# Mixture-of-experts blocks made of two half blocks of 32 slots, four weight slots in the ring, and a TensorE loop of one block

## The chip, the cores and the metric

The kernel runs on one core of a Trainium2 chip. The metric is the device time of one execution in microseconds (us), as the median of three runs. In the profile, PE is TensorE (PEld its weight loads, PEldq its sequencer's own instructions), DVE is VectorE, ACT ScalarE, POOL GpSimd and SP SyncE.

## The reference

A backbone of two layers works on 256 latent tokens and 256 context tokens of width 1024. Each layer has a token mixing part (windowed attention, a bidirectional state-space scan, a bidirectional gated recurrence and global attention, side by side) and a channel mixing part, which the change touches:

```python
scores = jax.nn.sigmoid((h @ router_w).astype(jnp.float32))
...
_, idx = lax.top_k(jnp.where(expert_mask, biased, -jnp.inf), TOP_K)
w = w / jnp.sum(w, axis=-1, keepdims=True) * ROUTED_SCALE
shared = (jax.nn.silu(h @ sh_gate) * (h @ sh_up)) @ sh_down
return routed_experts(h, idx, w, w_gate, w_up, w_down) + shared
```

Each token goes to 8 of 64 experts. An expert is `(silu(x @ w_gate) * (x @ w_up)) @ w_down` with a hidden width of 256, so it has 3 MB of f32 weights. The first layer routes 512 tokens, the second only the 256 latent ones, since only those are put out.

## The kernel before

After the routing, VectorE sorts the assignments of tokens to experts into blocks of 64 slots. A block holds tokens of one expert; an expert with 65 tokens takes two blocks, and what is left of its last block is empty. The table `TAB` holds the expert of every block, `PEND` the running sum of blocks by expert, and `NPR` the number of pairs of blocks. Each engine then runs a loop over pairs of blocks, whose two halves are written out (u = 0 and 1) so that each can use its own buffers: `OH`, `XGT`, `HIDT`, `YSB`, `XG`, and the banks 0/1 for up, 2/3 for down, 4/6 for turned tokens.

For block b the work runs as follows. VectorE builds a one-hot matrix of the block's slots (`one_hot`, L1631) from the table's expert. TensorE multiplies it with `KV` (`meta`, L1185), which gives token numbers and destinations. VectorE turns these into row numbers (`rows`, L1641). GpSimd gathers the token rows by an indirect DMA (L657), each token as two half rows, so that 64 slots fill 128 partitions. TensorE transposes them (`turn_tokens`, L1196), and ScalarE copies them to `XGT` (L885). TensorE multiplies them with the gate and the up weights (`up`, L1202: 8 chunks, the gate to partitions 0 to 63 and up to 64 to 127 of one bank, as two column groups of 64). ScalarE takes silu of the gate half (L891), VectorE multiplies (`product`, L1676), TensorE transposes the hidden rows (`turn_hidden`, L1225), ScalarE copies them (L902), TensorE multiplies with the down weights (`down`, L1217, two column groups of 64), ScalarE evicts (L907), and GpSimd scatters the rows to `yrows` (L676).

TensorE's order in the body is: `meta` of block b+3, up of b+1 with the hidden transpose of b inside it, the token transposes of b+2, down of b. Table loads (`expert_of`) and branches choose the ring slot of the expert, since addresses in the code are fixed: there is a copy of up and of down for each of the three slots (L1260 to L1278).

The weights arrive through a ring of three slots of 3 MB. Expert e lies in slot e % 3. SyncE loads gate, up and down of an expert (L521, L526) on one queue, in order of experts. In `reload` (L529) it waits until the last block of the expert in that slot is through up (`pe_gu`), issues the gate and up loads of the expert three further on, waits for its down (`pe_dn`), and issues the down load. One semaphore per slot counts the landings, and up waits for all three of them (`expert_landed`, L1213). All 64 experts are loaded, with tokens or not. The ring also serves the adaLN, projection and shared-expert weights before; expert 2's slot is the last to come free, after the shared expert's down.

Ahead of the loop VectorE counts blocks by expert in `NB` (L1608 to L1610), prepares blocks 0 to 2, and computes the tokens' expert weights `WK` and their diagonals `DG` (L1669, L1673) before the first `product`.

## Time and profile before

| | |
|---|---|
| median of 3 runs | 2148.57 us (2148.31 to 2156.99) |
| the profiled execution | 2138.5 us |
| its span | 2136.7 us |
| mean granted clock of TensorE in it | 0.948 of full speed |
| TensorE busy | 1835.1 us (86% of the span) |
| VectorE, ScalarE, GpSimd busy | 846.2, 542.0, 426.2 us |
| moved by DMA | 578.28 MB, mean 271 GB/s |

The busy times are of one profiled execution, so they are read against its span and not against the median. Busy shares are means over stages of different kinds; the two expert loops are stretches of their own in it. The idle time that a view gives ahead of a group of instructions is split by what ended it: a DMA, another engine's line, or "issue", when the engine waited for nothing that the profile shows.

### The profile page before, as it was taken

What the parts mean: (1) busy time and instruction counts of PE and PEld (TensorE: products, weight loads), DVE (VectorE), ACT (ScalarE), POOL (GpSimd) and SP (SyncE); (2) the same over time, 40 slices, a digit from 0 to 9 for tenths busy, and PEclk for the clock granted to TensorE, in tenths of its full rate; (3) what the DMA queues carried; (4) which work ended last, traced back from release to release, by engine and by line L of the source; (5) the groups of instructions that cost most, each with busy time, mean ns of one, the idle gap of its engine ahead of it and who ended that gap; (6) DMA issues with size and microseconds to landing.
All of it is one profiled execution on the core that took longest, in us unless ns stands there. A gap on an engine that the chain in (4) does not pass through costs nothing. (4 is left out here: it accounts for less than half of the span.)

```text
span 2136.7 us, 39465 instructions
## 1 busy us (share of the span) xinstructions
PE 1835.1 (86%) x11495; PEld 992.2 (46%) x11496; DVE 846.2 (40%) x2836; ACT 542.0 (25%) x1163; POOL 426.2 (20%) x417
## 2 busy tenths in 40 slices
PE   4999699879999999999997589879688887888885
PEld 3545454435445545445553355545444444444442
DVE  2245563363333333333334526543532323223334
ACT  2142352222222222222221214233222222222221
POOL 0001300012223223222321000130122222222220
PEclk8999899999999999999999889969799999999998
DMA  8315510449999789897985853631599999999994
GB/s 278 126 66 201 188 60 1 177 170 377 369 388 357 257 309 359 315 376 270 383 334 198 297 158 110 250 129 34 209 354 370 409 399 411 397 406 400 363 385 185
DMA packets 170400, 578.28 MB, mean 271 GB/s; under 512 B 29756, under 2 KB 34592, under 8 KB 153448
## 3 DMA queue, kind: packets, MB, share of 16 engines
q1 hardware_dynamic: 134592, 515.49, 62.7%
q0 software_dynamic: 29056, 60.07, 7.7%
q10 hardware_dynamic: 6696, 1.98, 0.4%
q8 instruction: 35, 0.57, 0.1%
q14 instruction: 21, 0.17, 0.0%
HBM read 565.73 MB, written 45.75 MB: 286 GB/s over the span
## 5 line engine op out<-in xcount | busy, mean ns | idle before, releaser
L1208 PE MATMUL bank<-arena 128*64 128x256 f32 x5120 | 643.0, 395 | 124.8 <-DMA arena<-in_exp_w_down 81.5
L1208 PEld LDWEIGHTS bank<-arena 128*64 128x64 f32 x5120 | 353.0, 140 | 293.1 <-DMA arena<-in_exp_w_down 86.8
L676 POOL DMA_INDIRECT yrows<-arena x158 | 160.3, 1014 | 832.8 <-ACT arena L907 814.7
L1221 PE MATMUL bank<-arena 128*64 128x512 f32 x1264 | 306.5, 606 | 0.7 <-issue 0.5
L657 POOL DMA_INDIRECT arena<-hrows,arena x164 | 185.9, 1133 | 144.3 <-DVE arena L1650 91.6
L1680 DVE TENSOR_TENSOR arena<-arena,bank 64x256 f32<-64x256 f32 x160 | 68.0, 425 | 353.9 <-ACT arena L891 353.8
L902 ACT ACTIVATE arena<-bank 128x128 f32<-128x128 f32 x158 | 44.2, 280 | 565.6 <-PE bank L1227 565.6
L907 ACT ACTIVATE arena<-bank 128x512 f32<-128x512 f32 x158 | 94.4, 597 | 210.1 <-PE bank L1221 210.1
L973 PE MATMUL bank<-arena 128*128 128x512 f32 (+3 forms) x384 | 133.9, 512 | 11.7 <-DVE arena L1337 11.7
L1645 DVE COPY arena<-bank 128x3 f32<-128x3 f32 x164 | 26.4, 161 | 288.9 <-PE bank L1192 288.3
L1199 PE MATMUL bank<-arena 128*128 128x128 f32 x648 | 121.9, 311 | 7.8 <-DMA arena<-hrows,arena 7.8
L1221 PEld LDWEIGHTS bank<-arena 128*64 128x64 f32 x1264 | 76.9, 136 | 110.7 <-issue 92.1
L1199 PEld LDWEIGHTS bank<-arena 128*128 128x128 f32 x648 | 90.9, 209 | 70.5 <-issue 61.2
L885 ACT ACTIVATE arena<-bank 128x512 f32<-128x512 f32 x162 | 96.8, 597 | 55.8 <-PE bank L1199 55.5
L973 PEld LDWEIGHTS bank<-arena 128*128 128x128 f32 x384 | 79.0, 217 | 64.8 <-issue 45.8
L1638 DVE TENSOR_TENSOR arena<-arena 128x512 bf16<-128x512 f32 (+1 forms) x166 | 97.9, 590 | 5.7
L976 PE MATMUL bank<-arena 128*128 128x512 f32 (+1 forms) x256 | 100.0, 552 | 0.0
L891 ACT ACTIVATE arena<-bank 64x256 f32<-64x256 f32 x160 | 60.2, 376 | 127.4 <-PE bank L1208 127.4
L1192 PEld LDWEIGHTS bank<-arena 128*128 128x128 bf16 x518 | 24.2, 97 | 133.3 <-issue 133.2
L1127 PE MATMUL bank<-arena 128*128 128x512 f32 x192 | 82.9, 593 | 1.0 <-DVE arena L1517 1.0
L1636 DVE TENSOR_SCALAR arena<-arena 128x4 f32 (+1 forms) x166 | 38.3, 231 | 108.1 <-issue 106.5
L1227 PEld LDWEIGHTS bank<-arena 64*128 64x128 f32 x316 | 48.9, 201 | 62.1 <-issue 62.1
(297 smaller groups left out, 1834.1 us busy)
## 6 DMA issues: line engine op xcount, KB each, us to landing
arena<-in_exp_w_gate SPq DMA_DIRECT2D x128, 1024.0 KB, 8.8
arena<-in_exp_w_up SPq DMA_DIRECT2D x128, 1024.0 KB, 11.1
arena<-in_exp_w_down SPq DMA_DIRECT2D x128, 1024.0 KB, 9.0
arena<-in_w_ada SPq DMA_DIRECT2D x10, 3072.0 KB, 13.7
arena<-yrows SPq DMA_DIRECT2D x24, 1024.0 KB, 16.3
arena<-in_w_ada SPq DMA_DIRECT2D x8, 2048.0 KB, 9.9
arena<-in_w_in SPq DMA_DIRECT2D x8, 2048.0 KB, 18.8
arena<-in_w_out SPq DMA_DIRECT2D x4, 2048.0 KB, 12.1
```

The lines of the kernel that those rows point to most:

```text
L657: pool.indirect_dma_start(out=XG[k], out_offset=None, in_=hrows, in_offset=bass.IndirectOffsetOnAxis(ap=GIX[k], axis=0), bounds_check=2 * ...
L676: pool.indirect_dma_start(out=yrows, out_offset=bass.IndirectOffsetOnAxis(ap=SIXS[u], axis=0), in_=YSB[u], in_offset=None, bounds_check=2 ...
L885: act.activation(XGT[b_par], bank[(4, 6)[b_par]][:, :].rearrange("p (c h s) -> p c h s", c=4, h=2), ACT.Copy).then_inc(a_xe, 1)
L907: act.activation(YSB[u], bank[2 + u][:, :], ACT.Copy).then_inc(a_y, 1)
L973: ins = pe.matmul(bank[o % 4][:, c0:width], HT[:, c, tile_of(j)], w[:, c, c0:], start=(c == 0), stop=(c == 7))
L976: ins = pe.matmul(bank[o % 4][:, c0:], w[:, c, tile_of(j)], HT[:, c, c0:], start=(c == 0), stop=(c == 7))
L1127: ins = pe.matmul(bank[2 * t + hf][:, :], MT[:, c, tile_of(t)], w[:, c, :], start=(c == 0), stop=(c == 7))
L1199: ins = pe.transpose(bank[(4, 6)[b_par]][:, c * P:(c + 1) * P], XG[b_par][:, c:512:4], IDENT)
L1208: ins = pe.matmul(bank[b_par][64 * gu:64 * gu + 64, 0:HID], XGT[b_par][:, c, hh, :], wv[:, gu, hh, c, :], start=(c8 == 0), stop=(c8 == 7))
L1221: ins = pe.matmul(bank[2 + b_par][64 * cg:64 * cg + 64, :], HIDT[b_par][:, c, :], wv[:, c, cg * 512:(cg + 1) * 512], start=(c == 0), stop= ...
L1638: dve.tensor_tensor(OH[par][:, T0:], IOTA.unsqueeze(1).broadcast_to([P, NTS, P]), RR[:, T0:].unsqueeze(2).broadcast_to([P, NTS, P]), ALU.i ...
L1680: dve.tensor_tensor(HIDB[64:128, :], HS[64:128, :], bank[par][64:128, 0:HID], ALU.mult).then_inc(v_hid, 1)
```

## The change

A block still has 64 slots, but it is now two units of 32 slots, each with an expert of its own. Tokens are rounded up to 32 per expert; an expert without tokens gets one unit. The number of blocks is half the number of units, rounded up to an even number. `TAB` holds the expert of each unit, and the new `TABK` the sum of the two experts of a block; since they are the same expert or neighbours, half the sum gives the first and the remainder the step to the second.

Up writes four column groups of 32 (gate and up of both units), down four as well (two halves of the output for both units), so each has twice the matmuls, of 32 stationary columns. `meta` writes two halves with a copied `KVP`, which `one_hot` fills on VectorE.

The ring has four slots, the fourth in the region of `H`, which is free once the rows have been stored. The down landings have a semaphore of their own (`sp_dn`), so up waits only for the gate and up parts. Experts 0, 1, 3, 2 are loaded ahead, 3 after the shared expert's up products and the store of the rows.

TensorE's loop holds one block for two. `OH`, `XGT`, `HIDT` and the banks 0, 2 and 4 are single now; up of b+1 waits for product(b) before it starts, and `turn_hidden` stands after 4 of the 8 chunks for 6. Each of up and down has eight copies: four slots, with or without a step.

```diff
-SLOTS = 64
+UNIT = 32
+SLOTS = 2 * UNIT
...
-        ring = [rRING + 6144 * k for k in range(3)]
+        ring = [rRING + 6144 * k for k in range(3)] + [rH]
...
                 def reload(i, u):
...
+                    units_up_to = sp.value_load(TABP[0:1, bass.ds(i * NSLOT + u, 1)], min_val=0, max_val=MAXU)
+                    used = sp.snap((units_up_to + 1) // 2)
+                    sp.wait_ge(sp_land[u], i * 32 + (base_land[u] + 32))
+                    sp.wait_ge(sp_dn[u], i * 16 + 16)
...
-                for e in range(3):
-                    sp.wait_ge(*done_of[P_OUT + e])
+                for e in (0, 1, 3, 2):
+                    if e < 3:
+                        sp.wait_ge(*done_of[P_OUT + e])
+                    else:
+                        sp.wait_ge(pe_sh, 4)
+                        sp.wait_ge(pool_hr, 16 * NTS)
                     load_up(e, e)
                     load_down(e, e)
...
                     for t in TS:
-                        ins = pe.matmul(bank[7][:, 0:3], OH[b_par][:, t, :], KV[:, t, bass.ds(e, 1), :].rearrange("p a c -> p (a c)"),
-                                        start=(t == T0), stop=(t == NT - 1))
+                        for un in range(2):
+                            ins = pe.matmul(bank[7][SLOTS * un:SLOTS * un + SLOTS, 0:3], OH[:, t, un, :], KVP[:, t, 3 * un:3 * un + 3],
+                                            start=(t == T0), stop=(t == NT - 1))
...
                         for gu in range(2):
-                            ins = pe.matmul(bank[b_par][64 * gu:64 * gu + 64, 0:HID], XGT[b_par][:, c, hh, :], wv[:, gu, hh, c, :],
-                                            start=(c8 == 0), stop=(c8 == 7))
+                            for un in range(2):
+                                r = 64 * gu + UNIT * un
+                                ins = pe.matmul(bank[0][r:r + UNIT, 0:HID], XGT[:, c, un, hh, :], wv[un][:, gu, hh, c, :],
+                                                start=(c8 == 0), stop=(c8 == 7))
...
                     for c in range(2):
-                        for cg in range(2):
-                            ins = pe.matmul(bank[2 + b_par][64 * cg:64 * cg + 64, :], HIDT[b_par][:, c, :], wv[:, c, cg * 512:(cg + 1) * 512],
-                                            start=(c == 0), stop=(c == 1))
+                        for un in range(2):
+                            for cg in range(2):
+                                r = 64 * un + UNIT * cg
+                                ins = pe.matmul(bank[2][r:r + UNIT, :], HIDT[:, c, UNIT * un:UNIT * un + UNIT],
+                                                wv[un][:, c, cg * 512:(cg + 1) * 512], start=(c == 0), stop=(c == 1))
                     ins.then_inc(pe_dn, 1)
+
+                def experts_of(b):
+
+                    both = pe.value_load(TABK[0:1, bass.ds(b, 1)], min_val=0, max_val=2 * NE - 2)
+                    e = pe.snap(both // 2)
+                    return e, pe.snap(e % NSLOT), pe.snap(both % 2)
+
+                def in_slots(slot, step, body):
+
+                    def pair(k):
+                        with pe.If(step == 0):
+                            body((k, k))
+                        with pe.Else():
+                            body((k, (k + 1) % NSLOT))
+
+                    with pe.If(slot == 0):
+                        pair(0)
+                    with pe.Else():
+                        with pe.If(slot == 1):
+                            pair(1)
...
+                blocks = pe.snap(pairs * 2)
+                with pe.Fori(0, blocks) as b:
+                    meta(b + 4, b + 3)
+                    e, slot, step = experts_of(b + 1)
+                    half = pe.snap(b // 2)
+                    odd = pe.snap(b % 2)
+                    pe.wait_ge(a_xe, b + 2)
+                    pe.wait_ge(v_hid, b + 1)
+
+                    def up_and_turn(ks):
+                        up_landed(e, ks)
+                        up(ks, range(0, 4), False)
+                        turn_hidden()
+                        up(ks, range(4, 8), True)
+
+                    in_slots(slot, step, up_and_turn)
+                    with pe.If(odd == 0):
+                        turn_tokens(0, half * 16 + 32)
+                    with pe.Else():
+                        turn_tokens(1, half * 16 + 32)
+                    now, slot_now, step_now = experts_of(b)
+                    pe.wait_ge(a_h, b + 1)
+                    pe.wait_ge(a_y, b + 2)
+
+                    def down_now(ks):
+                        down_landed(now, ks)
+                        down(ks)
+
+                    in_slots(slot_now, step_now, down_now)
...
-                for m in range(1, NTOK // SLOTS):
-                    link(dve.scalar_tensor_tensor(out=NB, in0=CNT, scalar=float(m * SLOTS), in1=NB, op0=ALU.is_gt, op1=ALU.add))
+                for m in range(1, NTOK // UNIT):
+                    link(dve.scalar_tensor_tensor(out=NB, in0=CNT, scalar=float(m * UNIT), in1=NB, op0=ALU.is_gt, op1=ALU.add))
+                link(dve.tensor_scalar(NB, NB, 1.0, None, ALU.max))
...
+                    es = [expert_of(b * 2 + un) for un in range(2)]
...
+                    for un in range(2):
+                        dve.tensor_copy(KVP[:, T0:, 3 * un:3 * un + 3], KV[:, T0:, bass.ds(es[un], 1), :].rearrange("p t a c -> p t (a c)"))
+                        ins = dve.tensor_scalar(RR[:, T0:, un:un + 1], GG[:, T0:, bass.ds(es[un], 1)], BASE[:, 0:1], None, ALU.subtract)
```

## Rows read from the trace of the kernel before

**Rows 1.** The page's DMA rate in 40 equal slices of the span.

```profile
GB/s 278 126 66 201 188 60 1 177 170 377 369 388 357 257 309 359 315 376 270 383 334 198 297 158 110 250 129 34 209 354 370 409 399 411 397 406 400 363 385 185
```

**Rows 2.** Up and down: count, ns min/median/max, first and last start (us).

```profile
L1208 PE MATMUL bank<-arena x2976: 379/379/689, 450.1 to 1142.5; 128*64 128x256 f32 x199
...
L1208 PE MATMUL bank<-arena x2144: 379/379/689, 1546.2 to 2094.0; 128*64 128x256 f32 x195
...
L1221 PE MATMUL bank<-arena x736: 592/592/1116, 468.1 to 1144.9; 128*64 128x512 f32 x184
```

**Rows 3.** Windows: PE, PEld, DVE, ACT, POOL busy (count), clock, DMA share, GB/s.

```profile
470.00:1146.00 676.00, 634.44 (x4554) 337.01 (x4550) 254.26 (x1001) 168.89 (x365) 195.99 (x182) 0.99 0.86 329
1552.00:2098.00 546.00, 467.41 (x3172) 243.08 (x3168) 166.17 (x727) 123.77 (x266) 140.88 (x131) 0.97 0.97 382
...
1583.00:2083.00 500.00, 425.87 (x2880) 221.41 (x2880) 150.33 (x659) 111.01 (x240) 129.26 (x120) 0.97 1.00 394
```

**Rows 4.** Idle ahead of L1208, window 470 to 1140 us: us, times.

```profile
  issue: 72.8, 142
  DMA arena<-in_exp_w_down: 17.0, 16
```

**Rows 5.** TensorE's timeline of one block: start, duration (us), line, count.

```profile
704.23 2.81 PE L1208 MATMUL bank<-arena 128*64 128x256 f32 x24 [0.35 <-issue]
706.97 0.45 PE L1227 MATMUL bank<-arena 64*128 64x64 f32 x2
707.35 1.08 PE L1208 MATMUL bank<-arena 128*64 128x256 f32 x8
708.36 0.75 PE L1199 MATMUL bank<-arena 128*128 128x128 f32 x4
709.04 1.94 PE L1221 MATMUL bank<-arena 128*64 128x512 f32 x8
710.91 0.25 PE L1192 MATMUL bank<-arena 128*128 x4
711.36 0.87 PE L1208 MATMUL bank<-arena 128*64 128x256 f32 x6 [0.19 <-issue]
```

**Rows 6.** adaLN matmuls (timeline), and full-array matmuls (group: busy us, mean ns).

```profile
26.20 3.68 PE L939 MATMUL bank<-arena 128*2 128x128 f32 x128
...
L973 PE MATMUL bank<-arena 128*128 128x512 f32 x192 | 84.4, 600 | 0.0
```

**Rows 7.** TensorE's sequencer: table loads, slot branches, the loop's back edge (L1243).

```profile
L1183 PEldq FUSED_REGOPS  x303: 46/151/151, 600.9 to 1094.5; - x152
L1183 PEldq TENSOR_LOAD <-arena x169: 296/305/1095, 601.0 to 1099.7; - x169
...
L1260 PEldq COMPARE_BRANCH  x89: 71/202/218, 600.5 to 1096.5; - x89
...
L1243 PEldq COMPARE_BRANCH  x34: 213/213/215, 610.3 to 1099.3; - x34
```

**Rows 8.** Timeline of layer 0's routing on DVE, and PE's first loop block.

```profile
431.86 1.78 DVE L1610 SCALAR_TENSOR_TENSOR arena<-arena 128x64 f32<-128x64 f32 x7
...
456.90 2.38 PE L1208 MATMUL bank<-arena 128*64 128x256 f32 x20 [2.91 <-issue]
463.61 1.12 PE L1208 MATMUL bank<-arena 128*64 128x256 f32 x4 [4.33 <-DVE arena L1680]
```

**Rows 9.** Queues (packets, MB, share): whole span; 450 to 480; 600 to 1140.

```profile
q8 instruction: 35, 0.57, 0.1%
...
q8 instruction: 4, 0.07, 0.8%
...
q1 hardware_dynamic: 32474, 148.86, 72.1%
q0 software_dynamic: 11680, 26.26, 13.2%
```

**Rows 10.** Layer 1's first up (timeline), and the window about it.

```profile
1546.24 6.06 PE L1208 MATMUL bank<-arena 128*64 128x256 f32 x32
...
1540.00:1560.00 20.00, 14.14 (x86) 7.79 (x86) 10.39 (x64) 4.11 (x7) 2.03 (x2) 0.74 0.67 261
```

More of the change, by code:

```diff
@@ L224, in build @@
         o = rXC
-        XGT = [at(o + 512 * k, 4, 2, SLOTS) for k in range(2)]; o += 1024
+        XGT = at(o, 4, 2, 2, UNIT); o += 512
         YSB = [at(o + 512 * k, 512) for k in range(2)]; o += 1024
         o = rXT
-        HIDT = [at(o + 128 * k, 2, SLOTS) for k in range(2)]; o += 256
-        SIXT = arena[:, o:o + TABN].bitcast(U32); o += TABN
+        HIDT = at(o, 2, SLOTS); o += 128
+        SIXT = arena[:, o:o + SIXN].bitcast(U32); o += SIXN
         SIXS = [arena[:, o + k:o + k + 1].bitcast(U32) for k in range(2)]; o += 2
@@ L235, in build @@
         NBH = at(o, 1); o += 1
-        RR = at(o, 4); o += 4
+        RR = at(o, NT, 2); o += 8
+        KVP = at16(o, NT, 6); o += 12
+        TABK = arena[0:1, o:o + SIXN].bitcast(I32); o += SIXN
+        EB2 = at(o, 2); o += 2
         BASE = at(o, 1); o += 1
@@ L262, in sem @@
             return s
-        sp_land = [sem(f"sp_land{k}") for k in range(3)]
+        sp_land = [sem(f"sp_land{k}") for k in range(NSLOT)]
+        sp_dn = [sem(f"sp_dn{k}") for k in range(NSLOT)]
         sp_yk = [sem(f"sp_yk{k}") for k in range(NYK)]
@@ L416, in landed @@
             return sp_land[k], 16 * sum(d for m, d in enumerate(dmas_of[:n + 1]) if slot_of(m) == k)
[L418 removed]
+        base_land = [16 * sum(d for m, d in enumerate(dmas_of) if slot_of(m) == k) for k in range(NSLOT)]
         with nc.Block() as block:
@@ new lines, in experts_of @@
+                def experts_of(b):
[14 more added lines that the diff above has]
+                        with pe.Else():
+                            with pe.If(slot == 2):
+                                pair(2)
+                            with pe.Else():
+                                pair(3)
@@ new lines, in _, with first_up @@
+                meta(3, 2)
+                _, _, step = experts_of(0)
+                pe.wait_ge(a_xe, 1)
+                def first_up(ks):
+                    up_landed(0, ks)
+                    up(ks, range(8), True)
+                with pe.If(step == 0):
+                    first_up((0, 0))
+                with pe.Else():
+                    first_up((0, 1))
+                turn_tokens(1, 16)
+                blocks = pe.snap(pairs * 2)
[14 more added lines that the diff above has]
+                        turn_tokens(0, half * 16 + 32)
+                    with pe.Else():
+                        turn_tokens(1, half * 16 + 32)
[6 more added lines that the diff above has]
+                    in_slots(slot_now, step_now, down_now)
@@ L1697, in _ @@
                         rows(1 - u, b + 3, SIXT[:, bass.ds(b + 3, 1)], chain)
-                        one_hot(u, b + 4, chain)
-                        product(1 - u, b + 2, b + 1)
+                        one_hot(b + 4, chain)
+                        product(b + 2, b + 1)
                         dve.wait_ge(pool_s[u], i * 16 + 16)
```

181 lines of the change are left out of this document (73 added, 108 removed).

## The prediction

> **What bounds the kernel now.** I read the page first, above all the DMA rate in 40 slices of 53 us [rows 1]. Two stretches hold most of the time, one expert loop per layer: the DMA rate runs at 350 or so with dips in the first, and flat near 400 GB/s in the second. The groups of the up matmuls (L1208) place them [rows 2]: 2976 instructions from 450 to 1142 us are (92 + 1) x 32, so 92 passes of the loop (the last multiplies nothing that is used); 2144 from 1546 to 2094 us are 66 + 1. Running the reference's routing on its inputs and rounding each expert's tokens up to 64 gives the same 92 and 66. The down matmuls (L1221) of layer 0 start 91 blocks apart from 468.1 to 1144.4 us [rows 2]: 7.43 us a block.
>
> The windows say what sets each pace [rows 3]. Layer 0: TensorE busy 634 of 676 us, DMA share 0.86: TensorE. Layer 1: TensorE 467 of 546 us, and from 1583 to 2083 us the DMA share is 1.00 at 394 GB/s: the expert loads. The idle time ahead of layer 0's up matmuls agrees: it is "issue", hardly a load [rows 4]. (These totals count the weight loads and the matmuls, so I halve them: 36 us of issue and 8 us of DMA, 0.40 and 0.09 us a block of layer 0.) A block of layer 0 in order of time [rows 5]: three quarters of up 2.74, hidden transpose 0.38, rest of up 1.01, token transposes 0.68, down 1.87, meta and gap 0.45, together 7.13 us, 6.94 without the 0.19 of issue. So fewer blocks pay in layer 0, and in layer 1 only what moves the loads pays.
>
> **Part by part: the count.** With the same token counts rounded to 32, each expert at least one unit, layer 0 has 158 units and layer 1 has 94; two to a block and an even number of blocks make 80 and 48, for 92 and 66 now. Every block still moves 128 half rows.
>
> **Array work of a block.** Up has 64 instructions for 32, each on 32 columns of the array instead of 64, down 16 for 8. If four column groups run at once, the stream time stays. The adaLN matmuls already write four groups of 32 partitions with four moving operands: 128 instructions of 128 columns took 3.68 us, 28.8 ns each, while a full-array matmul of 512 columns takes 84.4/192 = 440 ns, 110 ns for 128 columns [rows 6]. That is 3.8 at once. But they load two weight columns, here it is 32. Ideal here is 3.41/64 = 53 ns; I take 55, +0.1 us a block, and as bound the 28.8 ns above plus half of what 64 columns cost now at most (107/2), 82 ns, which would be +1.8 us. Down's instructions are twice as long, so I take its 1.87 as it is. Meta goes from 4 to 8 short matmuls, 4 x 28 ns = +0.1. Moving turn_hidden from after chunk 5 to after chunk 3 costs nothing. Sum 6.94 + 0.2 = 7.15.
>
> **Issue.** The sequencer's own work: a table load is 0.15 + 0.31 us, a compare and branch 0.07 to 0.2, the loop's back edge 0.21 [rows 7]. meta no longer loads the expert (-0.46 a block); the back edge comes every block, not every second (+0.11); four slots and a step need on average one more branch than three slots (+0.2), at up and again at down; the arithmetic on b and on the table word is some six more register operations at 0.05 (+0.3). Down's share hides behind the token transposes and the tail of up, since idle time stands before L1208. So about +0.1 ahead of up: 0.5 for 0.4. Bounds: 0.1 (all hidden, with the load gone) and 1.3 (0.4 and all that is added, 0.9). The pitch before waits for loads is 7.65.
>
> **Single buffers.** The up of block b+1 waits for product(b). Up(b) ends, silu 0.4, product 0.4; TensorE meanwhile has tokens 0.68, down 1.87 and meta 0.45: 3 us of cover for 0.9, so nothing. If VectorE comes late, up waits, and down, the slot release and the loads queue behind it. VectorE's chain grows by a second table load, two copies and one subtraction, some 1.2 us on about 3.2 after meta, against 4.6 to the end of up: covered too. Bank 2 is evicted 0.6 us after down and needed 5 us later; XGT likewise.
>
> **Prologue.** NB takes 15 comparisons for 7: 1.78/7 = 0.25 each [rows 8], +2.0 us, with TABK and the longer one_hots some +5 until product(0). Now the second up runs 20 of its instructions before it waits 4.33 us for that product [rows 8]; after, all of it follows the wait, at a cooled clock: +5 more. Layer 0: +10 (bounds 5 and 14).
>
> **Code.** The first jump into the loop stalled 2.91 us with nothing to wait for, and the instruction queue brought four packets between 450 and 480 us; between 600 and 1140 us the view lists no instruction packets at all [rows 8, 9]. 35 packets of 16 KB are 8960 instructions, which is TensorE's whole program, so today's loop (536 array instructions by the code, each f32 matmul as two loads and two matmuls, and some 80 others: 40 KB) stays resident. The new body has 8 variants of up (some 137 each), 8 of down (36), 16 + 16 of meta and tokens and some 100 others: about 1500, 94 KB, six packets. No row shows that 94 KB stay. I take that they do (the bound on the other side is the rival below), with two more cold stalls of 2.9 in layer 0, +6; in layer 1 they lie in the waits for loads.
>
> **Layer 0's loads.** 64 experts at 3.15 MB and 33.5 MB of gathered and scattered rows, at 394 GB/s, are 596 us, 62 experts of them after the routing: about 580. The loop needs 79 x 7.65 = 604. Close: single-unit experts let TensorE catch up with the loads, so waits stay, 0.1 a block as now. Layer 0: 79 x 7.75 = 612 against 91 x 7.43 = 676, -64, and +10 and +6: -48.
>
> **Layer 1.** The loads set the end: the bytes stay. The fourth slot lets one expert land during the routing, 3.15/0.394 = -8 us. Against it: the token counts give 19 of 48 blocks with two new experts. Such a block waits for 2 x (3.15 + 0.35) MB = 17.8 us of transfer with 7.7 of work, so TensorE idles 10 us. When its up weights have landed, the queue holds one down and one up part, 3.15 MB, 8 us; the next down load is issued only after up, tokens and down, 4.2 + 0.7 + 1.9 = 6.8 us. That fits at full clock. But after idle stretches this long 32 up instructions took 6.06 us, for the 3.75 of a block now [rows 5], the granted clock of that stretch being 0.74, part of it at 1.2 GHz, not 2.4 [rows 10]: 6.8 + 2.4 + issue leaves the queue empty for 1 us or so, 19 times less what overlaps: +10. Layer 1: +2 (bounds -18 and +20).
>
> **Sum.** -48 + 2 = -46; tails of the layers unchanged. The profiled execution took 2138.5 us (span 2136.7), the median is 2148.6, 10 above; the difference goes against the median: 2148.6 - 46 = 2103.
>
> **Rivals.**
> *Layer 0 runs near its bounds* (pitch 7.25, gap hidden): 79 x 0.5 = 40 more, and layer 1 gains its 8 to 18: about 2050. For it: a removed table load sits right where the gap is now. Against: the loads' floor of 580 us, which cuts it to some 25: 2070.
> *The sequencer eats the gain.* Break-even is at a pitch of 7.75 + 46/79 = 8.3 us, a gap of 1.1. Up now needs 128 issues in 3.5 us, 27 ns each, so less run-ahead is left for the branches; the adaLN rows show 14 ns an issue, which speaks against it. About 2145.
> *The code doesn't stay.* Every block jumps to an up variant, a down variant and back. One miss in a block at 2.9 us [rows 8] is 79 x 2.9 = +229 in layer 0, and in layer 1 mostly inside the waits: 2103 + 240 = 2343; three misses would give about 2950. It decides from one miss in five blocks of layer 0 on (46/229). For it: 94 KB have never been shown resident; against: 40 KB in three packets are, with jumps over variants all the time. The Trainium skill, "Runtime: NRT & Kernel Launch", section "Instruction fetch mechanics", says that a taken branch outside a window of two 16 KB pages forces a fetch; by that rule today's loop of three packets would fetch too, and the trace shows none. "Advanced Engine Details and Errata", section "ISA Cache", gives TensorE 128 KB, which would hold it; no run here shows that.
> *The column groups don't run four at once with real weights*: 82 ns, +1.8 us a block: 79 x 1.8 = +142, layer 1 +15: about 2260.
>
> **Chances.** Forecast (2075 to 2135) 0.52; faster still 0.15; sequencer, 2135 to 2165, 0.13, of which within 0.5% 0.08; code 0.12; columns 0.05; layer 1 slower by its cooled clock so that the whole loses 0.03. A measurement of this kernel tells about 0.5%, 11 us, from no change. Faster 0.70 (0.52 + 0.15 + the part of the sequencer's that stays below 2138, 0.03), same 0.09, slower 0.21. The range of 2050 to 2160 leaves out the code and column cases and a little below.
>
> **What would show it.** Blocks: L1221 in 80 + 48 = 128 blocks, 2048 instructions; pitch of layer 0 7.75; 64 up instructions in 3.5 to 3.7 us (columns wrong: over 5); idle before up "issue" 0.5 a block; idle before it on product(b) none; instruction packets none in mid-loop; layer 1's DMA share at 0.97 or more and TensorE's clock there below 0.9. The forecast falls if the instruction queue shows packets all through the loops, or if the last expert of layer 1 lands earlier or later than 540 us after its first up.

## The result: 5% slower

The kernel after took 2263.26 us (median of 4 runs, 2261.21 to 2268.72), the kernel before beside it 2152.24: ratio 1.0506, 95% interval 1.0482 to 1.053. Forecast were 2103 us and a chance of 0.70 for faster. The time is outside the range. The profiled execution took 2261.47 us, span 2259.7, so 123 us more span than the trace of the kernel before. That trace (2138.5 us) is as quick as the kernel before was on the quicker of two kinds of chip that the experiments show, and this result is from the slower kind; so, by the times of the kernel before, some 13 of the 123 us belong to the chips. The comparison within one kind stands at the end of "Empty instructions".

First the blocks. Up and down of the kernel after, from the view of one line; after the colon the shortest, median and longest in ns, then the first and last start in us:

```profile
L1222 PE MATMUL bank<-arena x5184: 376/379/636, 456.8 to 1228.8; 128*32 128x256 f32 x200
...
L1247 PE MATMUL bank<-arena x1280: 589/592/1062, 488.1 to 1232.4; 128*32 128x512 f32 x183
...
L1247 PE MATMUL bank<-arena x2048: 589/592/1062, 488.1 to 2219.5; 128*32 128x512 f32 x187
```

5184 is 81 x 64 and 1280 is 80 x 16: 80 blocks in layer 0, and 48 in layer 1, as forecast. But downs start 9.42 us apart ((1232.4 - 488.1)/79, 7.43 in [rows 2]). From the first up to the last down, layer 0 takes 775.6 us against 694.8; 68 of the 81 us are the pitch (79 x 9.42 against 91 x 7.43) and 13 the way in. Layer 1 takes 588 us (1631.2 to 2219.5) against 550: +38. That is 119 of the 123 us.

The windows of both loops (columns as in [rows 3]), and the timeline of one block (start, duration, in brackets the idle time ahead, us), to hold against [rows 5]:

```profile
600.00:1100.00 500.00, 396.30 (x5076) 196.03 (x5068) 173.65 (x755) 99.17 (x215) 109.79 (x108) 0.99 0.86 326
1640.00:2200.00 560.00, 363.75 (x4131) 171.85 (x4135) 135.23 (x647) 84.39 (x183) 92.51 (x91) 0.86 0.92 365
```

```profile
702.07 0.75 PE L1211 MATMUL bank<-arena 128*128 128x128 f32 x4
703.55 1.92 PE L1247 MATMUL bank<-arena 128*32 128x512 f32 x16 [0.73 <-issue]
705.40 0.29 PE L1204 MATMUL bank<-arena 128*64 128x3 bf16 x8
706.61 1.93 PE L1222 MATMUL bank<-arena 128*32 128x256 f32 x32 [0.92 <-issue]
708.47 0.45 PE L1278 MATMUL bank<-arena 64*128 64x64 f32 x2
708.85 2.17 PE L1222 MATMUL bank<-arena 128*32 128x256 f32 x32
710.96 0.75 PE L1211 MATMUL bank<-arena 128*128 128x128 f32 x4
```

In mid-loop TensorE was busy 94% of the time; it is 79% now at the same clock, while the DMA share stands at 0.86 as before. The matmuls are as quick as forecast: 32 up instructions in 1.93 us, so the four column groups run at once. What is new are two gaps in every block, one ahead of down, where none was, and one ahead of up. The groups of the window 600 to 1100 us, with busy us, mean ns, and the idle time ahead:

```profile
L1222 PE MATMUL bank<-arena 128*32 128x256 f32 x3456 | 223.8, 383 | 45.3 <-issue 41.1 <-DMA arena<-in_exp_w_up 3.6
L1247 PE MATMUL bank<-arena 128*32 128x512 f32 x864 | 107.2, 614 | 59.3 <-issue 59.3
```

864 downs are 54 blocks: 9.26 us each, 1.10 idle ahead of down and 0.84 ahead of up, nearly all "issue": no wait for another engine, and 3.6 us in all for loads.

What the sequencer does meanwhile. Its branches and its table load between the end of down's issue and the start of up's, 703.6 to 706.7 us (count, shortest/median/longest ns, first and last start), and two rows of the window 600 to 1100:

```profile
L1260 PEldq COMPARE_BRANCH  x2: 177/192/208, 703.7 to 706.2; - x2
L1300 PEldq COMPARE_BRANCH  x1: 222/222/222, 704.0 to 704.0; - x1
L1253 PEldq TENSOR_LOAD <-arena x1: 300/300/300, 704.6 to 704.6; - x1
L1265 PEldq COMPARE_BRANCH  x1: 207/207/207, 705.6 to 705.6; - x1
L1268 PEldq COMPARE_BRANCH  x1: 68/68/68, 705.9 to 705.9; - x1
...
L1260 PEldq COMPARE_BRANCH  x164: 66/169/216, 602.6 to 1094.7; - x164
...
L1253 PEldq TENSOR_LOAD <-arena x108: 297/302/815, 600.7 to 1099.2; - x108
```

The sequencer leaves down's code at 703.7, 0.1 us after down's first matmul: it has queued all 16. It reaches up at 706.6, 2.9 us later; down and meta are done in 2.1. The operations themselves are short, but some 0.06 us lies between any two of them. Its seven branch lines hold 569 compare-and-branches in 54 blocks, 10.5 a block; the five of the kernel before hold 353 in 67, 5.3.

### The profile page after: what moved, and what is told of

It reads as the page before. It is cut to its first block and busy times, and to the rows that moved or that the text cites. A ratio compares the mean times of both kernels' runs of the same rounds, so it can differ in the third digit from the quotient of the medians.

```text
span 2259.7 us, 47795 instructions
## 1 busy us (share of the span) xinstructions
PE 1691.9 (75%) x15651; PEld 877.1 (39%) x15652; DVE 829.8 (37%) x2930; ACT 485.9 (22%) x1043; POOL 346.6 (15%) x357
## 3 DMA queue, kind: packets, MB, share of 16 engines
q10 hardware_dynamic: 6696, 1.98, 0.4%
## 5 line engine op out<-in xcount | busy, mean ns | idle before, releaser
L1222 PE MATMUL bank<-arena 128*32 128x256 f32 x8320 | 571.5, 405 | 244.3 <-DMA arena<-in_exp_w_up 122.4
L1222 PEld LDWEIGHTS bank<-arena 128*32 128x32 f32 x8320 | 280.3, 115 | 424.1 <-issue 185.7
L1247 PE MATMUL bank<-arena 128*32 128x512 f32 x2048 | 252.8, 610 | 132.0 <-issue 131.8
L690 POOL DMA_INDIRECT yrows<-arena x128 | 129.7, 1013 | 1037.8 <-ACT arena L921 1037.8
L671 POOL DMA_INDIRECT arena<-hrows,arena x134 | 136.8, 1021 | 142.1 <-DVE arena L1704 100.7
L1247 PEld LDWEIGHTS bank<-arena 128*32 128x32 f32 x2048 | 60.2, 110 | 229.7 <-issue 228.6
L921 ACT ACTIVATE arena<-bank 128x512 f32<-128x512 f32 x128 | 76.4, 597 | 316.3 <-PE bank L1247 316.3
L1688 DVE COPY arena<-arena 128x12 bf16 (+1 forms) x272 | 67.6, 249 | 193.1 <-issue 193.1
L1211 PE MATMUL bank<-arena 128*128 128x128 f32 x528 | 99.1, 310 | 10.5 <-issue 9.5
L899 ACT ACTIVATE arena<-bank 128x512 f32<-128x512 f32 x132 | 78.8, 597 | 50.5 <-PE bank L1211 49.9
L1141 PE MATMUL bank<-arena 128*128 128x512 f32 x192 | 82.9, 593 | 1.0 <-DVE arena L1566 1.0
L1204 PEld LDWEIGHTS bank<-arena 128*64 128x64 bf16 x868 | 24.6, 111 | 126.3 <-issue 112.4
L1340 PE MATMUL bank<-arena 128*128 128x512 f32 x96 | 50.1, 654 | 30.2 <-DMA arena<-yrows 30.2
```

Source lines behind the costliest of these rows:

```text
L671: pool.indirect_dma_start(out=XG[k], out_offset=None, in_=hrows, in_offset=bass.IndirectOffsetOnAxis(ap=GIX[k], axis=0), bounds_check=2 * ...
L690: pool.indirect_dma_start(out=yrows, out_offset=bass.IndirectOffsetOnAxis(ap=SIXS[u], axis=0), in_=YSB[u], in_offset=None, bounds_check=2 ...
L899: act.activation(XGT, bank[4][:, :].rearrange("p (c u h s) -> p c u h s", c=4, u=2, h=2), ACT.Copy).then_inc(a_xe, 1)
L921: act.activation(YSB[u], bank[2][:, :], ACT.Copy).then_inc(a_y, 1)
L1141: ins = pe.matmul(bank[2 * t + hf][:, :], MT[:, c, tile_of(t)], w[:, c, :], start=(c == 0), stop=(c == 7))
L1211: ins = pe.transpose(bank[4][:, c * P:(c + 1) * P], XG[par][:, c:512:4], IDENT)
```

## The experiments

Theory S: the sequencer's work between its two stretches of matmuls is longer than what it has queued ahead. Rivals: loads, the single buffers, the ring, code that does not stay loaded.

One thing has to be known for all numbers. The five sets of runs (e1 to e4, e5 to e8, e9 to e12, e13 to e16, e17 to e19) fell on five chips, and the kernel before takes 2136 to 2137 us on two of them and 2150 to 2155 on three. I compare each run with the kernel before on its own chip, and call these chips of the first and of the second kind. Each chip served one set, so what belongs to the chip and what to the hour isn't told apart. e3 gave no time; e6 has its idea. A time is the median of 4 executions for the result, e17 and e18, of 5 for e13 and e19, and a single execution for the rest.

| run | us | before, same chip | kind of chip |
|---|---|---|---|
| after (the result) | 2263.3 | 2152.2 | second |
| e17, after again | 2258.8 | 2152.4 | second |
| e14, e15, e16 (= after) | 2272.6, 2266.1, 2266.5 | 2154.8 | second |
| e5, loop head placed | 2260.1 | 2150.4 | second |
| e9 (= after) | 2217.9 | 2135.8 | first |
| e1, one table load more | 2269.4 | 2137.2 | first |
| e2, the same in before | 2140.0 | 2137.2 | first |
| e4, no reloads | 2005.4 | 2137.2 | first |
| e6, tables under up | 2170.2 | 2150.4 | second |
| e7, e18, decoded under up | 2133.8, 2137.7 | 2150.4, 2152.4 | second |
| e13 (= e7) | 2138.2 | 2154.8 | second |
| e10 (= e7) | 2116.3 | 2135.8 | first |
| e8, two blocks in the loop | 3889.4 | 2150.4 | second |
| e11, before with ring of four | 2139.0 | 2135.8 | first |
| e12, before with loop of one | 2204.5 | 2135.8 | first |
| e19, ring of four, carried | 2079.1 | 2152.4 | second |

### One table load more, in both kernels

```
+ pe.value_load(TABK[0:1, bass.ds(b + 1, 1)], min_val=0, max_val=2 * NE - 2)
  pe.wait_ge(a_h, b + 1)
```

Its value is not used; in the kernel before it reads `TAB`.

> One more table load by TensorE's sequencer in every block of the changed kernel, ahead of down; its value is not used. Theory S (TensorE's sequencer sets the pace of layer 0: 0.8 us of its own work for a table load with its register operations, and the queue ahead of the array holds too few matmuls to hide it): layer 0's blocks go from 9.3 to 10.1 us, the whole gets 60 to 85 us longer, to about 2330. Rival theories (expert loads, single buffers or the column groups set the pace): at most 10 us longer.

> The same extra table load in every block of the kernel before. Theory S: its matmuls last 107 ns each and not 53, so the same queue hides it: within 5 us of the kernel before. If a sequencer operation always shows: 0.8 us on 92 blocks and some of layer 1, +75 to +90 us.

The kernel before took it for 3 us. The kernel after went to 2269.4, which looked like nothing against 2263, and I first read it as a miss of S. It was the comparison that was wrong: on a chip of the first kind the kernel after takes 2217.9 (e9, below), so the load cost 51 us, a little below what S expected. It lies open in one kernel and is covered in the other. (The two numbers are from two chips of the first kind, where the kernel before took 2137.2 and 2135.8.)

### No reloads

The loads of experts 4 to 63 are left out, and with them the arithmetic in the waits for landings; the blocks multiply whatever experts 0 to 3 left in the slots.

```
- pe.wait_ge(sp_land[k], e * 8 + (base_land[k] + 32 - 8 * k))
...
+ for n in sorted(set(ks)):
+     pe.wait_ge(sp_land[n], base_land[n] + 32)
```

> The changed kernel without the loads of experts 4 to 63: each block multiplies with the weights of the first four experts; branches, blocks and rows as before. Theory S: layer 0 keeps 9.2 to 9.3 us a block, layer 1 falls to 9.2 a block without waits (-145 us), the whole about 2110. If loads or their traffic set layer 0's pace, its blocks fall under 9 us as well.

2005.4, 212 us below the kernel after on such a chip. Most is layer 1 (first up to last down 410 us for 589; it has 46 blocks here, since layer 0 hands it other values). Layer 0 falls by 31 us only (694 for 726 from the same marks), the pitch from 8.79 to 8.40. The groups from 600 to 1100 us, 60 blocks:

```profile
L1204 PE MATMUL bank<-arena 128*32 128x256 f32 x3888 | 235.1, 382 | 43.2 <-issue 43.2
L1225 PE MATMUL bank<-arena 128*32 128x512 f32 x960 | 116.3, 597 | 33.0 <-issue 32.8
```

With no load at all the two gaps still stand, 0.72 ahead of up and 0.55 ahead of down, for 0.85 and 0.78 in e9, the kernel after on a chip of this kind. The loads do not make them. Part of the difference may be the sequencer's arithmetic in the waits, which went with the loads; that was not tried apart. The expectation missed the time (2110), and its pitch of 9.2 was that of a chip of the second kind; that pitches under 9 us would speak for the loads doesn't hold for the same reason.

### The tables, then all decoding, moved under up's matmuls

The sequencer is far ahead of the array while up's matmuls run, so by S work there should be free. e6 moves the table loads there, e7 also the division into expert, slot and step; registers carry the values to down and to the next up.

```
  up(ks, range(0, 2), False)
+ for to, of in ((r_dn, r_now), (r_now, r_next)):
+     for x, y in zip(to, of):
+         pe.reg_mov(x, y)
+ pe.reg_mov(r_half, b // 2)
+ pe.reg_mov(r_odd, b % 2)
  up(ks, range(2, 4), False)
  turn_hidden()
+ decode(b + 2, r_next)
  up(ks, range(4, 8), True)
```

> The kernel after with both table loads of a block replaced by one that stands among up's matmuls; the values go to down and to the next up in registers. The decoding into slot and step and all branches stay. S: about 0.6 us of the sequencer's work leaves each of the two gaps (ahead of down 1.0 us idle, ahead of up 0.75), so 1.2 us of a block: pitch 9.4 to 8.2 (7.6 if the supply of instructions recovers as well), time 2063 to 2130. Rival (the ring's loads or the single buffers set the pitch, the sequencer's work is covered): idle ahead of down stays, 2245 to 2270.

> As the run with the tables under up, and the decoding into expert, slot and step, the block's half and its parity are computed among up's matmuls as well and carried in registers; between the stretches only waits and branches are left, about 1.5 us ahead of down against 1.5 us of queued matmuls and 0.75 of transposes, and 1.9 us ahead of up against 2.1 us. S: idle ahead of down and up under 0.2 us each in layer 0, pitch 7.2 to 7.6, time 1990 to 2060, below the kernel before. Rival (buffers or loads set the pitch): not below 2200.

> The kernel with its decoding under up, unchanged, beside the kernel before: ratio 0.989 to 0.995, 2114 to 2122 on a chip of the first kind and 2132 to 2142 on one of the second.

2170.2, then 2133.8: 90 and 126 us below e5, which is the kernel after but for where its loop's head lies and ran beside them (2260.1), and e7 is below the kernel before; again as e18, ratio 0.9926, interval 0.9903 to 0.995. Buffers, ring, blocks and matmuls are those of the kernel after. So S holds. Both times missed their ranges (2063 to 2130 and 1990 to 2060): the pitch of the whole loop came to 8.29 and 7.93 from 9.43, nearly as expected for e6, but layer 1 gave back only 4 and 10 us. Whether the units pay is another question; e19 below answers it. e18's groups in the window 600 to 1000 us:

```profile
L1222 PE MATMUL bank<-arena 128*32 128x256 f32 x3264 | 213.7, 386 | 14.0 <-DMA arena<-in_exp_w_up 11.5 <-issue 1.5
L1247 PE MATMUL bank<-arena 128*32 128x512 f32 x816 | 98.1, 598 | 13.8 <-issue 13.2
```

51 blocks, 7.84 us each: "issue" has gone from 0.76 to 0.03 ahead of up and from 1.10 to 0.26 ahead of down. I expected 7.2 to 7.6; 0.23 of the rest are waits for loads, which the quicker loop now meets in layer 0 too.

### Empty instructions, and what they showed instead

In e1 and e4 up took 4.18 us in nearly every block, in the kernel after 4.48 on average. I took this for a matter of where the code lies: e5 puts the loop's head on a fixed place, e9, e14, e15 and e16 put 4, 4, 1 and 12 `pe.nop()` into the loop, e10 puts 4 into e7.

> The kernel after, with the first instruction of TensorE's block loop laid at the start of a fetch block; no work added or taken. Two theories of the missing time of a block. S: the sequencer's register and branch work between its two long stretches of matmuls is longer than the matmuls that it has queued ahead (idle ahead of down and of up, about 1.7 us a block). F: part of it is the supply of instructions inside up: the 64 instructions of up take up to 4.7 us in the kernel after, and 4.18 us in every block of the run with one table load more and of the run without reloads. If F's part hangs on where the code lies, up takes 4.18 us in all blocks, the pitch goes from 9.4 to 8.6 and the time to 2180 to 2210. If it does not hang on the head's place, 2255 to 2270.

> The kernel after with four empty instructions ahead of down's waits in TensorE's loop, which do nothing but stand where the extra table load of an earlier run stood: some 0.2 to 0.3 us of the sequencer's time a block. If the slow supply of instructions inside up (up takes 4.48 us there, and 4.18 with the extra table load) hangs on where the code behind it lies, up takes 4.18 us in all blocks, pitch 8.8, time 2195 to 2220. If it hung on the load's time, nothing recovers: 2275 to 2295. If the empty instructions are neither, 2255 to 2275.

> The kernel with its decoding under up (2133.78 us) with the same four empty instructions. If they mend the supply inside up there as well, up goes from 4.58 to 4.2 us, pitch from 7.85 to 7.3, time 2085 to 2110; if not, 2130 to 2150.

> The kernel after with four empty instructions ahead of up's waits, so that up's code and all behind it move. If the supply inside up depends on the lengths in the loop at either place, up 4.18 us and the time 2215 to 2235; if the place behind up matters, up stays at 4.48 us: 2280 to 2300 (the four cost 0.25 us ahead of up in each of 128 blocks).

> The kernel after with one empty instruction ahead of down's waits. If the recovery grows with the distance moved, part of it is left: 2235 to 2260. If any shift mends it, 2200 to 2215.

> The kernel after with twelve empty instructions ahead of down's waits: 0.7 to 0.8 us of the sequencer's time a block, on the path ahead of down. If the supply stays mended, up 4.18 us, pitch 9.2 to 9.3, 2265 to 2290; if twelve instructions bring the slow supply back, pitch over 9.8 and over 2320.

> The kernel after, unchanged. If the supply of instructions differs from chip to chip, the three times go together: where the kernel before takes 2135 to 2140, this one takes 2215 to 2225 with up at 4.18 us; where before takes 2150 to 2157, this one takes 2260 to 2270 with up at 4.5 us. If it belongs to the program, 2260 to 2270 everywhere.

> The decoded kernel with four empty instructions again, timed in five rounds against the kernel before: 2116 against 2136 to 2150, a ratio of 0.985 to 0.992, clearly under 1.

e9's 2217.9 looked like a cure by four empty instructions, and e10's 2116.3 too. Twelve cost nothing either, where the sequencer needs some 0.06 us between any two operations. The first line of each run's page of the profile says why. The kernel after, e9 and e16:

```profile
span 2259.7 us, 47795 instructions
```

```profile
span 2216.1 us, 47795 instructions
```

```profile
span 2264.7 us, 47795 instructions
```

The counts are the same, so by them the empty instructions are in none of the programs: these are the kernel after, on other chips. That is also why e14 (2272.6) and e15 (2266.1) fit neither reading of their expectations. The same program takes 2218 us on one chip and 2259 to 2273 on others, and e7, e10, e13 and e18 are one program at 2116 on the first kind and 2134 to 2138 on the second (e13: ratio 0.9921, interval 0.9905 to 0.9937). e17, the kernel after unchanged, took 2258.8 beside a kernel before of 2152.4, which is nearest to the second reading of its expectation. The unchanged source was not run on a chip of the first kind: e9's has the four lines of `pe.nop()`. e10 and e13, though, have one source to the letter, and took 2116.3 and 2138.2. e5's 2260.1 says that the place of the loop's head does nothing on such a chip. e9's groups in the window 600 to 1100:

```profile
L1222 PE MATMUL bank<-arena 128*32 128x256 f32 x3685 | 224.4, 384 | 49.4 <-issue 45.0 <-DMA arena<-in_exp_w_up 4.4
L1247 PE MATMUL bank<-arena 128*32 128x512 f32 x928 | 111.6, 597 | 45.5 <-issue 45.4
```

58 blocks of 8.62 us, with 3685 up instructions in 224.4 us, where the kernel after has 3456 in 223.8: 60.9 ns for 64.8, 0.25 us a block. The rest of the difference (0.64) is mostly the gap ahead of down, 0.78 for 1.10. e9's block in the timeline, and the branch that leaves its up:

```profile
702.69 1.93 PE L1222 MATMUL bank<-arena 128*32 128x256 f32 x32 [1.16 <-issue]
704.56 0.45 PE L1278 MATMUL bank<-arena 64*128 64x64 f32 x2
704.93 1.94 PE L1222 MATMUL bank<-arena 128*32 128x256 f32 x32
706.80 0.75 PE L1211 MATMUL bank<-arena 128*128 128x128 f32 x4
708.60 1.92 PE L1247 MATMUL bank<-arena 128*32 128x512 f32 x16 [1.05 <-issue]
```

```profile
L1262 PEldq COMPARE_BRANCH  x1: 169/169/169, 705.4 to 705.4; - x1
```

The sequencer leaves up at 705.4 and the array ends it at 706.87: a lead of 1.46 us, the same in most blocks of e1, e4 and e9 between 600 and 1100 us and 1.35 in nearly all others. In the kernel after that branch comes at 710.0 and up ends at 711.02: a lead of 1.0, as in most of its blocks (0.6 to 1.5 in all), and the second half of up takes 2.17 us, in other blocks up to 2.5, for 1.93. So on chips of the second kind the instructions of up come more slowly at times, which costs array time and lead. Why those chips do so stays open; the instruction queue moved no packet there. It is 13 to 19 us of the kernel before, and 40 or more of the kernel after, which has twice the matmuls in up and down. The loss against the kernel before is 82 us on a chip of the first kind and 106 to 118 on one of the second.

Within the first kind the loss is made up otherwise than the first reading above. e9's downs of layer 0:

```profile
L1247 PE MATMUL bank<-arena x1280: 589/592/1061, 489.4 to 1183.8; 128*32 128x512 f32 x183
```

Their pitch is 8.79 us, so the loop takes 79 x 8.79 = 694 us for 676: the two gaps ate the gain of the fewer blocks and 18 us more. The way in costs 13, layer 1 39 (589 for 550), and layer 0's first up comes 8 us later. Together that is 78 of the 79 us by which e9's span is longer. Half of the loss is layer 1's.

### Two blocks in the loop

> The kernel after with two blocks in TensorE's loop as in the kernel before: no branch on the parity, no halving, one back edge for two blocks; the code of the loop doubles to about 190 KB. S alone, if all of it stays loaded: 0.4 us of a block less, 2205 to 2225. If a loop of that size does not stay loaded: packets of the instruction queue throughout the loop, idle of several us ahead of up in every block, over 2600.

```
- with pe.Fori(0, blocks) as b:
+ with pe.Fori(0, pairs) as i:
+     for u in range(2):
+         b = i * 2 + u
```

3889 us. Its timeline, and its instruction queue over the whole span (packets, MB, share); the kernel after has 45 packets there, and none from 600 to 1200 us:

```profile
909.42 0.29 PE L1204 MATMUL bank<-arena 128*64 128x3 bf16 x8
923.12 3.34 PE L1222 MATMUL bank<-arena 128*32 128x256 f32 x32 [13.41 <-issue]
...
931.78 2.64 PE L1247 MATMUL bank<-arena 128*32 128x512 f32 x16 [2.40 <-issue]
939.61 0.38 PE L1204 MATMUL bank<-arena 128*64 128x3 bf16 x8 [5.19 <-issue]
952.32 3.64 PE L1222 MATMUL bank<-arena 128*32 128x256 f32 x32 [12.33 <-issue]
```

```profile
q8 instruction: 789, 12.93, 1.5%
```

Twice the code does not stay loaded, and most blocks fetch again: 12 to 13 us ahead of up in the two shown, 2 to 19 in the whole run, nearly all of it in single branches (6.7 and 5.3 us of the 13.41). The loop of one block, which looked like a cost, is what lets this change run at all: some 94 KB stay, some 190 KB do not (sizes by the prediction's count). The Trainium skill, "Advanced Engine Details and Errata", section "ISA Cache", gives TensorE 128 KB; both runs agree. By the window of two pages in the Trainium skill, "Runtime: NRT & Kernel Launch", section "Instruction fetch mechanics", the kernel after would fetch throughout; the trace shows that it does not.

### The parts of the change, alone, in the kernel before

e11: the ring of four slots with down's landings counted apart. e12: TensorE's loop of one block with single buffers. Both keep the blocks of 64 slots and one expert.

```
- ring = [rRING + 6144 * k for k in range(3)]
+ ring = [rRING + 6144 * k for k in range(3)] + [rH]
```

```
- with pe.Fori(0, pairs) as i:
-     for u in range(2):
...
+ blocks = pe.snap(pairs * 2)
+ with pe.Fori(0, blocks) as b:
```

> The kernel before (blocks of 64 slots with one expert, loop of two blocks, double buffers) with the ring of four slots and the landings of down's weights counted apart. S: the ring has no part in the loss: layer 0's pitch 7.4 to 7.7 (one more slot to branch to), layer 1 at 530 to 560 us as before, time 2130 to 2175. Rival (the fourth slot and the second count cost what the kernel after lost): over 2200.

> The kernel before with TensorE's loop of one block and single buffers, blocks of 64 slots with one expert and three ring slots. Its matmuls last 107 ns, so what is queued ahead lasts twice as long. S: idle ahead of down under 0.2 us, ahead of up 0.3 to 0.9 us (back edge, table load, branches against the 2.2 us of down and the slot matmuls), pitch 7.5 to 8.1, time 2150 to 2230. Rival B (single buffers bring the loss): TensorE waits for ScalarE or VectorE in each block, pitch over 8.5, over 2260.

e11 took 3 us more than before: layer 0 15 us longer (0.17 us a block, with one more branch), layer 1 14 us shorter, 536 us at a DMA share of 0.97. e12 took 69 us more. Its groups, 600 to 1100 us:

```profile
L1208 PE MATMUL bank<-arena 128*64 128x256 f32 x1984 | 241.5, 385 | 67.0 <-issue 65.9 <-DMA arena<-in_exp_w_down 1.1
L1221 PE MATMUL bank<-arena 128*64 128x512 f32 x496 | 120.1, 605 | 1.6 <-issue 1.6
```

62 blocks, 8.06 us: 1.1 us of "issue" ahead of up (0.3 to 0.9 expected), next to nothing ahead of down, and no wait for ScalarE or VectorE. So single buffers cost nothing in mid-loop, as forecast; the loop of one alone costs 0.6 us a block, since the back edge, a table load and the branches lie between down and up of every block. The gap ahead of down needs what the units bring as well. e12's lead at up's end is 1.8 to 1.9 us in every block, that of the units 1.46; and e12 has 7.2 branches a block for 10.5. No run takes the shorter lead and the added branches apart.

### A better kernel

e19 takes the ring of four and the carrying, without units and without the loop of one: the expert is loaded once a block under up for all three uses.

```
+ pe.reg_mov(rD, rE[0])
+ pe.reg_mov(rSD, rS[0])
+ pe.reg_mov(rS[0], rS[1])
+ pe.reg_mov(rS[1], pe.snap(rE[2], min_val=0, max_val=NE - 1) % 4)
+ for n in range(3):
+     pe.reg_mov(rE[n], rE[n + 1])
  up(1 - u, k, range(3, 5), False)
+ pe.reg_mov(rE[3], expert_of(b + 4))
```

> The kernel before (blocks of 64 slots, one expert each, loop of two blocks) with the ring of four slots and with the experts and slots of the next blocks loaded and decoded once a block under up and carried in registers. By S the idle ahead of up in layer 0 (0.3 to 0.5 us a block) goes: pitch 7.15 to 7.25, 92 blocks, so layer 0 20 to 28 us shorter; by the reading of layer 1 (its loads set it, and blocks that take two new experts at once stop the transfers more) layer 1 keeps the 14 us that the ring of four gave: ratio to before 0.978 to 0.987. Rival (layer 1's loss in the kernels with units is the ring's): layer 1 over 560 us, ratio 0.99 to 1.01.

2079.1 us, ratio 0.9666, interval 0.9646 to 0.9687. Its group of up, 600 to 1000 us, and layer 1's window:

```profile
L1215 PE MATMUL bank<-arena 128*64 128x256 f32 x1836 | 223.7, 385 | 0.2
```

```profile
1500.00:2036.00 536.00, 459.54 (x3202) 240.75 (x3204) 169.63 (x751) 123.50 (x266) 141.16 (x131) 0.99 0.97 386
```

57.4 blocks, 6.97 us each, no idle time. Layer 1 took 534 us for 550 and layer 0 652 for 695. It beat its expectation: I had taken 0.2 to 0.3 us off a block, and it gave 0.46, all the idle time there was ahead of up, waits for loads of down included. The kernel before in the window 600 to 1100, 68 blocks:

```profile
L1208 PE MATMUL bank<-arena 128*64 128x256 f32 x2170 | 265.8, 387 | 29.8 <-issue 23.6 <-DMA arena<-in_exp_w_down 6.0
```

The ratio is also from a chip of the second kind, where the kernel before loses 13 to 19 us; e19's up takes 4.20 us in every block there, so it seems to lose none of it. It was not run on a chip of the first kind.

e19 also says what the units are worth. e18 has the same ring and the same carrying, with units and the loop of one, on the same chip: 2137.7 us for 2079.1. Layer 0 takes the same time in both (653 and 652 us), as the pitch of 7.89 and a way in of 30 us use up what twelve blocks fewer give; layer 1 takes 579 us for 534. So the kernel with units is a little faster than the kernel before thanks to the ring and the carrying, and the units, with the loop of one that comes with them, cost 58 us.

## Why the prediction was wrong

**Right.** The counts, the four column groups at once, the array work of a block (7.15 forecast; 8.62 less 1.63 idle is 6.99 on a chip of the first kind), no wait on product(b) in mid-loop, no packets in mid-loop, layer 1's clock below 0.9 (0.86). Its DMA share was to be 0.97 and was 0.92.

**The step that failed is "Issue"**: "Down's share hides behind the token transposes and the tail of up", with 0.5 us ahead of up. Measured: 1.10 ahead of down and 0.84 ahead of up, so a pitch of 9.42 for 7.75, 79 x 1.67 = 132 us of the 169 that separate forecast and profile. Some 50 of the 132 come from the kind of chip, which no term of the prediction had. On a chip of the first kind (e9) the gaps are 0.78 and 0.85 and the pitch is 8.79: 82 us of the 128 between the forecast of 46 less and the measured 82 more. Two things were taken wrongly. I counted added operations at their own duration and a few of them; they are 5 more branches and their arithmetic, and each operation brings 0.06 us of gap. The table loads fell by half a load a block (169 in 67 blocks, 108 in 54) and not by the whole one of meta, since the kernel before loaded for down in every second block only. And I took the cover from the kernel before, whose lead with matmuls of some 105 ns is 1.9 us (e12), for matmuls of some 50 ns ((1.93 - 0.38)/31), with which it is 1.46 on a chip of the first kind and 1.0 on one of the second. With 0.68 of token transposes that covers 2.1 us at best; the sequencer needs 2.8 to 2.9. So nothing ahead of down is covered any longer, and what is added comes out nearly in full, as one more table load shows (51 us against 3). How much is due to the added branches and how much to the shorter lead stays open.

**The rival "the sequencer eats the gain"** was the right mechanism. I held 14 ns an issue against it, which is beside the point: the issues are quick, the branches between them are not. Its break-even of 8.3 us a block was too high, since it took layer 1 at +2: e6, at 8.29, took 2170 beside 2150; e7 and e18, at 7.9, are under the kernel before.

**Prologue and code, +16 in layer 0.** Measured +13 from the first up to the first down, and 7 more until that first up. The mechanisms were right. The second up has 14.43 us of idle time ahead of it, of which the first 9 are the wait for product(0), as forecast, and one branch that took 3.85 us. The view puts all of it down to "issue", since the branch came last. Layer 0, with the product that up waits for, the sequencer's branch and the up, and then the same for layer 1:

```profile
472.79 0.42 DVE L1732 TENSOR_TENSOR arena<-arena,bank 64x256 f32<-64x256 f32 x1
...
L1265 PEldq COMPARE_BRANCH  x1: 3849/3849/3849, 473.5 to 473.5; - x1
...
477.90 3.64 PE L1222 MATMUL bank<-arena 128*32 128x256 f32 x32 [14.43 <-issue]
...
1640.38 0.42 DVE L1732 TENSOR_TENSOR arena<-arena,bank 64x256 f32<-64x256 f32 x1
...
L1265 PEldq COMPARE_BRANCH  x1: 5437/5437/5437, 1641.0 to 1641.0; - x1
L1268 PEldq COMPARE_BRANCH  x1: 3060/3060/3060, 1646.5 to 1646.5; - x1
...
1650.35 3.64 PE L1222 MATMUL bank<-arena 128*32 128x256 f32 x32 [13.17 <-issue]
```

In layer 1 the wait for product(0) ends at 1640.8, and the two branches take 8.5 us. The instruction queue has packets around both and none in mid-loop.

**Layer 1, +2 (bounds -18 to +20), measured +38**, and not by the gaps: the decoded kernel on a chip of the first kind (e10) has 0.4 us of idle time ahead of down in all of layer 1, and the layer still takes 582 us, at a DMA share of 0.90:

```profile
1491.00:2073.00 582.00, 377.69 (x4385) 173.86 (x4388) 149.62 (x729) 90.97 (x195) 97.57 (x96) 0.81 0.90 358
```

The ring is not the cause: with blocks of 64 it made layer 1 14 us shorter (e11, e19). That leaves the units and the loop of one. The term that failed is the way in. I had hidden its stalls in waits for loads, but the four slots were full by then, so the transfers stood still as well. The kernel after, 15 us about that stall (DMA share and GB/s last):

```profile
1647.00:1662.00 15.00, 9.61 (x90) 4.14 (x90) 0.98 (x5) 1.85 (x4) 0.00 (x0) 0.70 0.02 5
```

The queue with the weights moves nothing for 16.7 us there, 14.2 in e10, against 4.4 in e11. After that it stands still six times, for 1 to 4 us and 15 to 16 in sum, in both kernels with units, and never in e11. The first of the six (from 1690 us on) follows a block that had waited 11.7 us for its loads; two slots came free together only after its down. That is the forecast's mechanism for blocks with two new experts, at 15 us for its +10. The two kinds of standstill are 26 of the 45 us between e10 and e11. What the rest is stays open.

## What to carry to other kernels

Before splitting blocks into more and shorter matmuls, look at how far the sequencer is ahead when TensorE ends its long stretch, and add up the sequencer's work up to the next one: the lead in microseconds falls with the matmuls' length, and once it is used up each branch or table load counts nearly in full, in each iteration. Work of the sequencer belongs among the matmuls, one block ahead, with the values carried in registers. Try that on the old kernel too before crediting the new one: here it gave more there. Where a gap is put down to "issue", look at the sequencer's own rows, since a wait and a slow branch can share it. And compare a run with the old kernel on the same chip only; a difference of 2% between chips passed twice for an effect here.

## What the runs showed of the hardware

- One program (47,795 instructions) took 2218 us on one chip and 2259 to 2273 on others, at the same granted clock (0.91 to 0.92) and with the same median matmul durations; the second half of its up was stretched from 1.93 us to up to 2.5.
- A loop of some 94 KB of TensorE's code ran in mid-loop without an instruction packet; one of some 190 KB had 789 packets in the run for 45, and 2 to 19 us of idle time ahead of up in most blocks.
- At the first entry into a loop single compare-and-branches took 3.85 us (layer 0) and 5.44 and 3.06 us (layer 1), for 0.07 to 0.22 in mid-loop; in the kernel before one took 1.98 us.
- The sequencer's lead at the end of up was 1.46 us with matmuls of some 50 ns and 1.8 to 1.9 us with matmuls of some 105 ns.
- Four matmuls on 32 columns each, with 32 columns of weights, kept the pace of two on 64: 64 up instructions in 4.18 us with the hidden transposes, for 32 in the same time.
